# Constant loads spread behind weight chunks, a norm weight applied inside ACT and DVE instructions, and the low-part copies cut differently around the norms

## The chip, the cores and the metric

One core of a Trainium2 chip runs the whole program in one launch. The metric is the device time of one execution in microseconds (us). Engine names are those of the profile: PE is the matrix engine (PEld its weight loads), DVE the vector engine, ACT the scalar engine, POOL the GpSimd engine, SP the engine whose queue issues nearly all transfers.

## What is computed

Four transformer layers over 256 rows of width 1024, all in float32. Cut to the parts that matter here:

```python
def rmsnorm(x, g):                    # two norms a layer in the first two layers
    y = x * rsqrt(mean(x * x, -1) + 1e-6)
    return y * g                      # g: one weight per column

for layer in (0, 1):                  # first block
    x = x + mixer(rmsnorm(x, norm_mix_g[layer]))      # stages 0 and 2
    h = rmsnorm(x, norm_ffn_g[layer])
    x = x + (silu(h @ w1) * (h @ w3)) @ w2            # stages 1 and 3
x = rmsnorm(x, final_norm_g)
for layer in (0, 1):                  # second block
    x = layer_norm(1.414 * x + attention(x), ...)     # stages 4 and 6
    x = layer_norm(1.414 * x + swiglu_2(x), ...)      # stages 5 and 7
```

Every stage is a row of large products of the 256 x K activations with weight matrices read from memory once.

## The kernel before

**Products.** A float32 product is made of three passes over fp32r operands. Each activation and each weight is split into a high part and a low part (low = value minus high), and PE adds high x high, low x high (lines 1020, 1021) and high x low (line 1027) into the PSUM banks `G`.

**Weight chunks.** Weights come in chunks of 128 partitions x 1024 columns (512 KB; three chunks of stage 0 are 840, 840 and 560 wide). Chunk `c` goes through three steps on three engines: SP loads it into one of 4 buffers `raw` (line 905), ACT copies it to one of 6 buffers `whi` (`split`, line 1902, named `HI` in the order), and POOL makes `wlo = raw - whi` (`lo`, line 2156). SP may load chunk `c` when POOL has finished chunk `c - 4`; ACT may split chunk `c` when PE has finished chunk `c - 6`. POOL cuts a chunk into pieces: 256 columns in the even stages, the whole 1024 columns in the odd ones.

```python
cuts = list(range(0, n, 256 if CHUNK_STAGE[c] % 2 == 0 else 1024)) + [n]
```

**Units.** PE's work is numbered in units: one chunk for one half `t` of the rows (two k-tiles, six matmuls of 512 columns). Within a block of output columns PE does all chunks for `t` = 0 and then all of them for `t` = 1.

**The order of everything else** is a table written by hand, `PLAN`, one text for each stage. `66: XG 0 0; SQ 1 0` means that after unit 66 every engine that owns such a step has it next in its queue. A leading minus means that the step belongs to the norm of the stage before. Each engine works strictly in this order, so a step that waits holds up all that stands behind it on its engine, the chunk splits on ACT among them.

**The norms of stages -1 to 2** (before the products of stages 0 to 3), for column half `b` and row half `t`: `RES` (DVE, line 1361) adds the product to `X`; `SQ` (ACT, 1926) sums squares; `XT` (PE, 1041) transposes four 128 x 128 tiles of `X` into the PSUM tensor `A`; `XG` (DVE, 1377) multiplies by the weight column in `CP` and writes to the SBUF buffer `W`; `XH` (ACT, 1943) copies `W` to the high part `xh`; `XL` (DVE, 1385) makes `xl = W - xh`; `SS` (DVE, 1368) and `RS` (ACT, 1885 and 1887) make the reciprocal root, which is applied later, when a product is read out (`EV`, line 1915, or `SI`, line 1956). For the layer norms of stages 4 to 7 there is no `XG`: `AP` (DVE, lines 1409 and 1413) has applied everything to `X` in SBUF, and `XH` and `XL` read `A`. The first unit of a stage waits for `XL 0 0`, the third for `XL 1 0`, the fifth for `XL 0 1`, the seventh for `XL 1 1`.

**Constants.** Behind the load of chunk 7, SP issues seven loads of constants in a row (lines 919 to 925): the two halves of `w1c`, three of `w2c`, the tables `CN` and the decay table in `LC`. `QT` (PE, line 1073) turns the first projected block for its row half, after `EV` of that half.

## Time and profile before

| | |
|---|---|
| time, median of 3 runs | 1406.63 us (1405.68 to 1406.87) |
| the profiled execution's own time | 1401.13 us |
| its span, first to last instruction | 1398.9 us |
| PE busy | 1342.9 us, 96% of the span |
| POOL busy | 1040.7 us, 74% |
| ACT busy | 706.6 us, 51% |
| DVE busy | 410.7 us, 29% |
| mean granted clock of PE | 0.987 of full |

How to read it: the profiled execution took 5.5 us less than the median of the runs (1406.63 less 1401.13), and 2.2 us of it lie outside its span (1401.13 less 1398.9). Times in the rows are counted from the span's start. In a row of the timeline the bracket at the end is the idle time of the engine just before the row, and what ended it.

### The profile page before, as it was taken

To read this page: it belongs to the slowest core of one execution; us is meant where nothing else is said; L and a number is where in the kernel's file an instruction comes from. 1 tells how busy PE (TensorE), PEld (TensorE's weight loads), DVE (VectorE), ACT (ScalarE), POOL (GpSimd) and SP (SyncE) were. 2 spreads that over 40 slices of the span, in tenths; PEclk is the share of its full clock that TensorE was granted. 3 is DMA by queue.
4 is the path that set the end of the run, shared out by engine and by line. 5 is a ranking of instruction groups with operands and counts; after the bars stand their busy time and mean duration, and the time that the engine had idled before them with its cause. 6 is when DMAs were issued, how large, how long until landed. Compare 5 with 4: busy or idle time off the path is not lost.

```text
span 1398.9 us, 19514 instructions
## 1 busy us (share of the span) xinstructions
PE 1342.9 (96%) x7598; PEld 1099.3 (79%) x7598; DVE 410.7 (29%) x785; ACT 706.6 (51%) x1193; POOL 1040.7 (74%) x827
## 2 busy tenths in 40 slices
PE   5999999999999999999999998899999999899997
PEld 4888778888877777888887777688887788688886
...
GB/s 258 100 68 100 125 168 204 182 193 170 193 171 93 121 77 121 194 183 181 181 189 162 185 133 121 139 215 187 195 176 190 192 139 162 111 220 182 191 173 88
DMA packets 63114, 224.90 MB, mean 161 GB/s; under 512 B 7344, under 2 KB 7984, under 8 KB 63024
## 3 DMA queue, kind: packets, MB, share of 16 engines
...
q10 hardware_dynamic: 288, 0.10, 0.0%
...
## 4 chain that ended last, share of the span: by engine, by line
PE 86%; POOL 4%; DVE 3%; ACT 3%; issue 2%; DMA 1%; SPq 0%; DVEq 0%; ACTq 0%
PE G L1020 24%; PE G L1021 24%; PE G L1027 24%; POOL wlo L2156 4%; PE A L1199 1%; PE A L1051 1%; ACT whi L1902 1%; PE A L1133 1%; DMA raw<-in_w_e 1%; PE G L1199 1%; PE A L1169 1%; PE A L1265 1%; DVE X L1409 1%; DVE X L1413 1%; PE G L1133 1%
## 5 line engine op out<-in xcount | busy, mean ns | idle before, releaser
L2156 POOL TENSOR_TENSOR wlo<-raw,whi 128x256 fp32r<-128x256 f32 (+2 forms) x819 | 1031.0, 1296 | 340.2 <-ACT whi L1902 340.2
L1902 ACT ACTIVATE whi<-raw 128x1024 fp32r<-128x1024 f32 x403 | 425.5, 1060 | 353.3 <-PE G L1027 326.6
L1020 PE MATMUL G<-whi,xh 128*128 128x512 f32 (+2 forms) x1200 | 465.8, 392 | 10.9 <-DVE xl L1385 7.1
L1021 PE MATMUL G<-whi,xl 128*128 128x512 f32 (+2 forms) x1200 | 452.7, 381 | 0.0
L1027 PE MATMUL G<-wlo,xh 128*128 128x512 f32 (+2 forms) x1200 | 352.4, 380 | 3.7 <-POOL wlo L2156 3.7
L1020 PEld LDWEIGHTS G<-whi,xh 128*128 128x128 f32 x1200 | 228.6, 190 | 55.7 <-ACT whi L1902 9.7
L1021 PEld LDWEIGHTS G<-whi,xl 128*128 128x128 f32 x1200 | 229.0, 191 | 38.3
L1027 PEld LDWEIGHTS G<-wlo,xh 128*128 128x128 f32 x1200 | 219.5, 190 | 49.7 <-POOL wlo L2156 6.1
L1020 PE MATMUL G<-whi,hh 128*128 128x512 f32 x352 | 139.4, 396 | 0.0
L1021 PE MATMUL G<-whi,hl 128*128 128x512 f32 x352 | 138.8, 394 | 0.0
L1027 PE MATMUL G<-wlo,hh 128*128 128x512 f32 x352 | 110.4, 395 | 0.0
L1361 DVE SCALAR_TENSOR_TENSOR X<-X,G 128x512 f32<-128x512 f32 x32 | 21.6, 685 | 228.8 <-PE G L1027 228.8
L1027 PEld LDWEIGHTS G<-wlo,hh 128*128 128x128 f32 x352 | 66.3, 188 | 15.4
L1021 PEld LDWEIGHTS G<-whi,hl 128*128 128x128 f32 x352 | 66.3, 188 | 15.0
L1020 PEld LDWEIGHTS G<-whi,hh 128*128 128x128 f32 x352 | 66.4, 189 | 15.0
L1426 DVE TENSOR_TENSOR sa<-G,sa 128x512 f32<-128x512 f32 (+1 forms) x24 | 15.5, 646 | 171.0 <-PE G L1027 171.0
L1423 DVE SCALAR_TENSOR_TENSOR sa<-G,SM,sa 128x512 f32<-128x512 f32 (+1 forms) x24 | 16.9, 706 | 163.2 <-PE G L1027 163.2
L1434 DVE TENSOR_TENSOR hl<-A,hh 128x512 fp32r<-128x512 f32 (+1 forms) x48 | 31.1, 647 | 95.7 <-ACT hh L1964 95.7
L1020 PE MATMUL G<-whi,mh 128*128 128x512 f32 x128 | 52.7, 412 | 2.4 <-DVE ml L1441 1.5
L1021 PE MATMUL G<-whi,ml 128*128 128x512 f32 x128 | 50.8, 397 | 0.0
L1027 PE MATMUL G<-wlo,mh 128*128 128x512 f32 x128 | 40.7, 399 | 0.0
L1964 ACT ACTIVATE hh<-A 128x512 fp32r<-128x512 f32 (+1 forms) x48 | 26.5, 552 | 15.2 <-PE A L1051 15.2
...
## 6 DMA issues: line engine op xcount, KB each, us to landing
...
```

The costliest lines, as they stand in the source:

```text
L1020: e.matmul(o, sh[:, kt, xs], whi[h][:, ws], start=u.first and j == 0, stop=False)
L1021: e.matmul(o, sl[:, kt, xs], whi[h][:, ws], start=False, stop=False)
L1027: m = e.matmul(o, sh[:, kt, xs], wlo[h][:, ws], start=False, stop=u.stop and final)
L1133: m = e.matmul(tile[:, at:at + nk], qs[i], ks[i], start=not mask, stop=True, skip_group_check=True)
L1199: m = e.matmul(tile[:, ow * i:ow * i + ow], w[1][0:kp, at:at + 128], vs[i][b], start=b == 0, stop=b == nb - 1)
L1361: e.scalar_tensor_tensor(out=x, in0=x, scalar=1.0 if st < 4 else ALPHA, in1=G[b][:, 512 * t:512 * t + 512], op0=ALU.mult, op1=ALU.add).the ...
L1423: e.scalar_tensor_tensor(out=s_, in0=ps, scalar=rstd[st - 1, t], in1=s_, op0=ALU.mult, op1=ALU.mult).then_inc(S["HM"], 1)
L1426: e.tensor_tensor(s_, ps, s_, ALU.mult).then_inc(S["HM"], 1)
L1434: e.tensor_tensor(hl[sl], ps, hh[sl].bitcast(F), ALU.subtract).then_inc(S["HL"], 1)
L1902: e.activation(whi[c % NH][:, 0:n], raw[c % NR][:, 0:n], ACT.Copy).then_inc(s_hi, 1)
L1964: e.activation(hh[:, 4 * b:4 * b + n, 128 * t:128 * t + 128], ps, ACT.Copy).then_inc(S["HH"], 1)
L2156: m = e.tensor_tensor(wlo[c % NH][:, i:j], raw[c % NR][:, i:j], whi[c % NH][:, i:j].bitcast(F), ALU.subtract)
```

## The change

It has three parts. The seven constant loads are taken apart: one goes behind each of the chunks 7, 8, 10 and 14 and three small ones behind chunk 9. `XG` is gone: in the norms with a weight, ACT reads the transposed tile in PSUM and multiplies by the weight as its per-partition scale, in four instructions of 128 columns, and DVE makes the low part in four instructions (`A * weight - xh`). The table's lines at the norms are written anew for that. And POOL takes chunks 0 to 7 whole, and the first six chunks of every odd stage in pieces of 256.

```diff
@@ PLAN, stage 0 @@
--1: -XT 0 0; -SQ 0 0; -XT 1 0; -XG 0 0; -SQ 1 0; -XG 1 0; -XH 0 0; -SS 0; HI 0; -XL 0 0; HI 1; HI 2
-0: -XH 1 0; -RS 0; -XL 1 0; -XT 0 1; -SQ 0 1; -XT 1 1; -XG 0 1; HI 3
-1: -XG 1 1; -XH 0 1; -XH 1 1; -XL 0 1; -SQ 1 1; -XL 1 1
-2: HI 4; -SS 1; -RS 1; HI 5
+-1: -XT 0 0; -SQ 0 0; -XT 1 0; -XH 0 0; -XH 1 0; -XL 0 0; HI 0; -XL 1 0; HI 1; HI 2
+0: -SQ 1 0; -SQ 0 1; -SS 0; -XT 0 1; HI 3; -XT 1 1
+1: -XH 0 1; -XH 1 1; -XL 0 1; -RS 0; -XL 1 1
+2: -SQ 1 1; HI 4; -SS 1; -RS 1
+3: HI 5
...
@@ SP, behind the load of chunk c @@
                 if c == 7:
+                    e.dma_start(CN[:, 128:NCONST], a["consts"][:, 128:NCONST]).then_inc(d_cn, 16)
+                if c == 8:
                     e.dma_start(w1c[:, 0, :], a["cw1k"]).then_inc(d_cw, 16)
-                    e.dma_start(w1c[:, 1, :], a["cw1v"]).then_inc(d_cw, 16)
+                if c == 9:
                     e.dma_start(w2c[:, 0:64], a["cw2k"]).then_inc(d_cw, 16)
                     e.dma_start(w2c[:, 64:128], a["cw2k"]).then_inc(d_cw, 16)
                     e.dma_start(w2c[:, 128:192], a["cw2v"]).then_inc(d_cw, 16)
-                    e.dma_start(CN[:, 128:NCONST], a["consts"][:, 128:NCONST]).then_inc(d_cn, 16)
+                if c == 10:
+                    e.dma_start(w1c[:, 1, :], a["cw1v"]).then_inc(d_cw, 16)
+                if c == 14:
                     e.dma_start(LC[:, 0:1024], a["ret"]).then_inc(d_ret, 16)
...
@@ DVE @@
-            def x_gain(key):
-                st, b, t = key
-                ps = heads4(A[t][:, 512 * b:512 * b + 512], 4)
-                tmp = heads4(W[t][b][:, 0:512], 4)
-                at = GAIN[st] + 4 * b
-                e.wait_ge(d_cp, 16)
-                e.wait_ge(S["XT"], nth("XT", *key))
-                e.tensor_tensor(tmp, ps, CP[:, at:at + 4].unsqueeze(2).to_broadcast([128, 4, 128]),
-                                ALU.mult).then_inc(S["XG"], 1)
...
+                if norm_kind(st) == "gain":
+                    for j in range(4):
+                        at, kt = GAIN[st] + 4 * b + j, 4 * b + j
+                        m = e.scalar_tensor_tensor(out=xl[:, kt, sl[2]], in0=A[t][:, 512 * b + 128 * j:512 * b + 128 * j + 128],
+                                                   scalar=CP[:, at:at + 1], in1=xh[:, kt, sl[2]].bitcast(F), op0=ALU.mult,
+                                                   op1=ALU.subtract)
...
@@ ACT @@
-                    e.wait_ge(S["XG"], nth("XG", *key))
-                    e.activation(oh, heads4(W[t][b][:, 0:512], 4), ACT.Copy).then_inc(S["XH"], 1)
+                    e.wait_ge(d_cp, 16)
+                    for j in range(4):
+                        at, kt = GAIN[st] + 4 * b + j, 4 * b + j
+                        m = e.activation(xh[:, kt, 128 * t:128 * t + 128], A[t][:, 512 * b + 128 * j:512 * b + 128 * j + 128],
+                                         ACT.Copy, scale=CP[:, at:at + 1])
...
@@ POOL @@
-                cuts = list(range(0, n, 256 if CHUNK_STAGE[c] % 2 == 0 else 1024)) + [n]
+                short = CHUNK_STAGE[c] % 2 == 0 and c >= 8 or CHUNK_STAGE[c] % 2 and c < FIRST[CHUNK_STAGE[c]] + NH
+                cuts = list(range(0, n, 256 if short else 1024)) + [n]
```

Three places of the instruction order follow. The first is SP's queue at the program's start, before the change, from the load of chunk 4 (the number behind `raw` is the buffer's).

```order
L905 DMA raw0<-in_w_e 128x1024
L905 DMA raw1<-in_w_e 128x1024
L905 DMA raw2<-in_w_e 128x1024
L905 DMA raw3<-in_w_e 128x1024
L919 DMA w1c<-in_cw1k 128x1024
L920 DMA w1c<-in_cw1v 128x1024
L921 DMA w2c<-in_cw2k 64x64
L922 DMA w2c<-in_cw2k 64x64
L923 DMA w2c<-in_cw2v 64x64
L924 DMA CN<-in_consts 128x1312
L925 DMA LC<-in_ret 128x1024
L905 DMA raw0<-in_w_e 128x840
```

The same queue with the change (lines count three more there); `in_ret` comes four chunks after the last row.

```order
L908 DMA raw3<-in_w_e 128x1024
L922 DMA CN<-in_consts 128x1312
L908 DMA raw0<-in_w_e 128x840
L924 DMA w1c<-in_cw1k 128x1024
L908 DMA raw1<-in_w_e 128x840
L926 DMA w2c<-in_cw2k 64x64
L927 DMA w2c<-in_cw2k 64x64
L928 DMA w2c<-in_cw2v 64x64
L908 DMA raw2<-in_w_e 128x560
L930 DMA w1c<-in_cw1v 128x1024
L908 DMA raw3<-in_w_e 128x1024
```

Chunks 8 and 9 (the two of 840 columns) now stand ahead of all constants but `CN` and one half of `w1c`.

The second place is DVE at the norm between stages 0 and 1, before the change: residual sums, `XG`, `SS`, the two `XL` of the first row half, the residual sums of the second half and its norm.

```order
L1361 SCALAR_TENSOR_TENSOR X<-X,G1 128x512
L1377 TENSOR_TENSOR W00<-A0,CP 128x512
L1368 TENSOR_TENSOR SM<-SM 128x1
L1377 TENSOR_TENSOR W01<-A0,CP 128x512
L1385 TENSOR_TENSOR xl<-W00,xh 128x4x128
L1385 TENSOR_TENSOR xl<-W01,xh 128x4x128
L1361 SCALAR_TENSOR_TENSOR X<-X,G0 128x512
L1361 SCALAR_TENSOR_TENSOR X<-X,G1 128x512
L1377 TENSOR_TENSOR W10<-A1,CP 128x512
L1377 TENSOR_TENSOR W11<-A1,CP 128x512
```

The same place with the change:

```order
L1368 SCALAR_TENSOR_TENSOR X<-X,G1 128x512
L1387 SCALAR_TENSOR_TENSOR xl<-A0,CP,xh 128x128 x4
L1375 TENSOR_TENSOR SM<-SM 128x1
L1387 SCALAR_TENSOR_TENSOR xl<-A0,CP,xh 128x128 x4
L1368 SCALAR_TENSOR_TENSOR X<-X,G0 128x512
L1368 SCALAR_TENSOR_TENSOR X<-X,G1 128x512
L1387 SCALAR_TENSOR_TENSOR xl<-A1,CP,xh 128x128 x8
L1375 TENSOR_TENSOR SM<-SM 128x1
```

The four `XG` are gone, and each `XL` is four short instructions that read PSUM (`A0`, `A1`) and `xh` instead of the two SBUF tensors `W` and `xh`.

The third place is POOL at the turn from stage 0 to stage 1; the turns into stages 3, 5 and 7 look alike. Before the change, the last chunk of stage 0 and the first ones of stage 1:

```order
L2156 TENSOR_TENSOR wlo4<-raw2,whi4 128x256 x4
L2156 TENSOR_TENSOR wlo5<-raw3,whi5 128x1024
L2156 TENSOR_TENSOR wlo0<-raw0,whi0 128x1024
L2156 TENSOR_TENSOR wlo1<-raw1,whi1 128x1024
L2156 TENSOR_TENSOR wlo2<-raw2,whi2 128x1024
L2156 TENSOR_TENSOR wlo3<-raw3,whi3 128x1024
```

With the change:

```order
L2168 TENSOR_TENSOR wlo5<-raw3,whi5 128x256 x4
L2168 TENSOR_TENSOR wlo0<-raw0,whi0 128x256 x4
L2168 TENSOR_TENSOR wlo1<-raw1,whi1 128x256 x4
L2168 TENSOR_TENSOR wlo2<-raw2,whi2 128x256 x4
L2168 TENSOR_TENSOR wlo3<-raw3,whi3 128x256 x4
L2168 TENSOR_TENSOR wlo4<-raw0,whi4 128x256 x4
L2168 TENSOR_TENSOR wlo5<-raw1,whi5 128x1024
```

Six chunks are in four pieces each, and the seventh is whole again.

## Rows read from the trace of the kernel before

**Rows 1.** Windows: start:end, length; busy us of PE, PEld, DVE, ACT, POOL; PE clock

```profile
180.00:200.00 20.00, 19.32 (x94) 15.64 (x93) 12.83 (x14) 14.05 (x25) 12.44 (x6) 1.00 0.50 155
200.00:366.00 166.00, 166.00 (x798) 138.58 (x797) 22.48 (x30) 78.33 (x89) 141.05 (x60) 1.00 0.61 188
866.00:890.00 24.00, 19.60 (x79) 14.74 (x78) 18.78 (x22) 9.21 (x14) 10.28 (x4) 0.89 0.28 87
1185.00:1215.00 30.00, 23.99 (x101) 18.43 (x100) 18.78 (x22) 12.23 (x17) 13.94 (x7) 0.94 0.33 102
```

**Rows 2.** PE's waits over the whole span: us in total, times, longest

```profile
PE G L1020 <- DVE xl L1385: 7.1, 4, 2.4
PE A L1041 <- DVE X L1413: 5.9, 7, 1.8
PE A L1073 <- ACT PJ L1915: 5.7, 1, 5.7
```

**Rows 3.** Timeline at the start: SP's queue, POOL, ACT and PE

```profile
22.07 0.43 SPq L919 DMA_DIRECT2D w1c<-in_cw1k  x1
...
9.23 23.52 POOL L2156 TENSOR_TENSOR wlo<-raw,whi 128x256 fp32r<-128x256 f32 x32 [8.79 <-ACT whi L1902]
21.73 0.72 PE L1027 MATMUL G<-wlo,xh 128*128 128x512 f32 x2 [1.10 <-POOL wlo L2156]
32.90 0.90 ACT L1902 ACTIVATE whi<-raw 128x840 fp32r<-128x840 f32 x1 [6.13 <-DMA raw<-in_w_e]
35.49 1.11 PE L1073 MATMUL A<-CN,PJ 128*128 128x128 f32 x4 [5.74 <-ACT PJ L1915]
36.26 0.77 PE L1020 MATMUL G<-whi,xh 128*128 128x512 f32 x1
```

**Rows 4.** The weight loads issued between 15 and 40 us, to landing

```profile
DMA to landing us min/median/max: 3.4/3.8/6.8
```

**Rows 5.** POOL's low-part instructions by shape, whole span (busy us, mean ns)

```profile
L2156 POOL TENSOR_TENSOR wlo<-raw,whi 128x1024 fp32r<-128x1024 f32 x264 | 632.0, 2425 | 158.8 <-ACT whi L1902 158.8
L2156 POOL TENSOR_TENSOR wlo<-raw,whi 128x256 fp32r<-128x256 f32 x552 | 398.5, 761 | 181.4 <-ACT whi L1902 181.4
```

**Rows 6.** The tile xl: its DVE instructions, ns min/median/max

```profile
L1385 DVE TENSOR_TENSOR xl<-W,xh x16: 678/1166/2723, 6.8 to 568.5; 128x512 fp32r<-128x512 f32 x16
L1385 DVE TENSOR_TENSOR xl<-A,xh x16: 639/680/693, 751.3 to 1206.0; 128x512 fp32r<-128x512 f32 x16
```

**Rows 7.** Timeline at the turn from stage 0 to stage 1, DVE

```profile
184.41 3.51 DVE L1385 TENSOR_TENSOR xl<-W,xh 128x512 fp32r<-128x512 f32 x2
```

**Rows 8.** Timeline at the start of stage 2

```profile
374.55 38.13 POOL L2156 TENSOR_TENSOR wlo<-raw,whi 128x256 fp32r<-128x256 f32 x48 [1.78 <-ACT whi L1902]
395.38 0.73 PE L1027 MATMUL G<-wlo,xh 128*128 128x512 f32 x2 [1.02 <-POOL wlo L2156]
```

**Rows 9.** Timeline at the turns into stage 5 and stage 7

```profile
871.92 2.58 DVE L1413 SCALAR_TENSOR_TENSOR X<-X,SM,LC 128x512 f32<-128x512 f32 x1 [0.39 <-ACT SM L1887]
877.52 2.08 DVE L1409 SCALAR_TENSOR_TENSOR X<-X,SM,LC 128x512 f32<-128x512 f32 x1
877.63 0.53 PE L1020 MATMUL G<-whi,xh 128*128 128x512 f32 x1 [2.42 <-DVE xl L1385]
1201.66 0.66 PE L1041 MATMUL A<-CN,X 128*128 128x128 f32 x4 [1.83 <-DVE X L1413]
```

**Rows 10.** DVE's norm instructions at the turn into stage 6, ns min/median/max

```profile
L1413 DVE SCALAR_TENSOR_TENSOR X<-X,SM,LC x4: 1037/1042/1048, 1068.1 to 1077.1; 128x512 f32<-128x512 f32 x4
L1409 DVE SCALAR_TENSOR_TENSOR X<-X,SM,LC x4: 744/986/1229, 1067.2 to 1075.7; 128x512 f32<-128x512 f32 x4
```

**Rows 11.** Instructions of 128 columns elsewhere in the kernel, on DVE and on ACT

```profile
L1834 DVE SCALAR_TENSOR_TENSOR MX<-A,SM,AG x10: 341/344/351, 784.8 to 861.9; 128x128 f32<-128x128 f32 x10
...
L2008 ACT ACTIVATE W<-A,SM 128x128 f32<-128x128 f32 x24 | 8.5, 366 | 9.9 <-DVE SM L1524 9.9
409.93 2.64 ACT L2083 ACTIVATE QK<-A 128x512 f32<-128x512 f32 x13
```

More of the change, by code:

```diff
@@ L208 @@
 SPLIT_AT = split_after()
+FIRST = [UNITS[BEGIN[st]].chunk for st in range(8)]
 def frees(kind, key):
@@ L290 @@
 65: RES 0 0; SQ 0 0; XT 0 0; RES 1 0
-66: XG 0 0; SQ 1 0; XT 1 0; XH 0 0; SS 0
-67: XG 1 0; XL 0 0; XH 1 0
+66: XH 0 0; SQ 1 0; XL 0 0; XT 1 0
+67: SS 0; XH 1 0
 68: XL 1 0
-69: RS 0; RES 0 1; XT 0 1; RES 1 1
+69: RES 0 1; RS 0; XT 0 1; RES 1 1
 """,
 """
-0: -SQ 0 1; -XG 0 1; -XT 1 1
-1: -XH 0 1; -XG 1 1; -SQ 1 1; -XL 0 1
-2: -XH 1 1; -SS 1; -RS 1; -XL 1 1
+0: -XH 0 1; -SQ 0 1; -XL 0 1; -XT 1 1
+1: -XH 1 1
+2: -SQ 1 1; -XL 1 1
+3: -SS 1; -RS 1
 4: SI 0 0
@@ L342 @@
 106: RES 0 0; SQ 0 0; XT 0 0
-107: XG 0 0; XH 0 0
+107: XH 0 0
 108: XL 0 0
 110: RES 0 1; SQ 0 1; XT 0 1
-111: XG 0 1; XH 0 1
-112: XL 0 1
+111: XH 0 1; XL 0 1
 128: RES 1 0; SQ 1 0; XT 1 0
-129: XG 1 0; SS 0; XH 1 0
+129: SS 0; XH 1 0
 130: XL 1 0
@@ L354 @@
 0: -RES 1 1; -XT 1 1; -SQ 1 1
-1: -XG 1 1; -SS 1; -XH 1 1
+1: -XH 1 1; -SS 1
 2: -RS 1; -XL 1 1
@@ L412 @@
 75: RES 0 0; SQ 0 0; XT 0 0; RES 1 0
-76: XG 0 0; SQ 1 0; XT 1 0; XH 0 0; SS 0
-77: XG 1 0; XL 0 0; XH 1 0
+76: XH 0 0; SQ 1 0; XL 0 0; XT 1 0
+77: SS 0; XH 1 0
 78: XL 1 0
-79: RS 0; RES 0 1; XT 0 1; RES 1 1
+79: RES 0 1; RS 0; XT 0 1; RES 1 1
 """,
 """
-0: -SQ 0 1; -XG 0 1; -XT 1 1
-1: -XH 0 1; -XG 1 1; -SQ 1 1; -XL 0 1
-2: -XH 1 1; -SS 1; -RS 1; -XL 1 1
+0: -XH 0 1; -SQ 0 1; -XL 0 1; -XT 1 1
+1: -XH 1 1
+2: -SQ 1 1; -XL 1 1
+3: -SS 1; -RS 1
 4: SI 0 0
@@ L700 @@
 SIGNALS = {
-    "EV": "block_evicted", "XT": "x_turned", "XG": "x_gained", "XH": "x_hi", "XL": "x_lo", "RES": "residual_added",
+    "EV": "block_evicted", "XT": "x_turned", "XH": "x_hi", "XL": "x_lo", "RES": "residual_added",
     "SQ": "squares_summed", "SS": "halves_summed", "RS": "rstd_ready", "BN": "bn_stats", "AG": "bn_aggregated",
@@ L1368, in sum_halves @@
                 e.tensor_tensor(norm_sum[key], m[:, 0:1], m[:, 1:2], ALU.add).then_inc(S["SS"], 1)
[L1370 to L1378 removed]
             def x_lo(key):
                 st, b, t = key
[L1382 removed]
                 sl = (slice(None), slice(4 * b, 4 * b + 4), slice(128 * t, 128 * t + 128))
                 e.wait_ge(S["XH"], nth("XH", *key))
[L1385 removed]
+                if norm_kind(st) == "gain":
[4 more added lines that the diff above has]
+                                                   op1=ALU.subtract)
+                else:
+                    m = e.tensor_tensor(xl[sl], heads4(A[t][:, 512 * b:512 * b + 512], 4), xh[sl].bitcast(F), ALU.subtract)
+                m.then_inc(S["XL"], 1)
             def layer_stats(key):
@@ L1854, in lam_ready @@
                 e.tensor_scalar(lam[:, 5:6], lam[:, 4:5], LAM0, None, ALU.add).then_inc(S["P3"], 1)
-            steps = {"RES": residual, "SS": sum_halves, "XG": x_gain, "XL": x_lo, "BN": layer_stats,
+            steps = {"RES": residual, "SS": sum_halves, "XL": x_lo, "BN": layer_stats,
                      "AG": layer_aggregate, "AP": apply_norm, "HM": gate_times_up, "HL": hidden_lo, "ML": mixed_lo,
@@ L1939, in x_hi @@
                 st, b, t = key
-                oh = xh[:, 4 * b:4 * b + 4, 128 * t:128 * t + 128]
+                e.wait_ge(S["XT"], nth("XT", *key))
                 if norm_kind(st) == "gain":
-                    e.wait_ge(S["XG"], nth("XG", *key))
-                    e.activation(oh, heads4(W[t][b][:, 0:512], 4), ACT.Copy).then_inc(S["XH"], 1)
-                else:
-                    e.wait_ge(S["XT"], nth("XT", *key))
-                    e.activation(oh, heads4(A[t][:, 512 * b:512 * b + 512], 4), ACT.Copy).then_inc(S["XH"], 1)
+                    e.wait_ge(d_cp, 16)
[3 more added lines that the diff above has]
+                                         ACT.Copy, scale=CP[:, at:at + 1])
+                else:
+                    m = e.activation(xh[:, 4 * b:4 * b + 4, 128 * t:128 * t + 128],
+                                     heads4(A[t][:, 512 * b:512 * b + 512], 4), ACT.Copy)
+                m.then_inc(S["XH"], 1)
             def gate_silu(key):
```

2 lines of the change are left out of this document (removed).

## The prediction

> **What bounds the kernel now.** I read the windows first, then PE's waits, then the timeline where a wait stands. In the body of an odd stage PE is busy 166.00 of 166.00 us at full clock: there PE alone is the bound, and nothing that this change does to other engines can be seen. Time is lost in short stretches around the norms: PE is idle for 0.68 us in 180:200, for 4.40 us in 866:890 and for 6.01 us in 1185:1215, in the last two with a mean clock of 0.89 and 0.94 [rows 1]. The list of PE's waits names the same places (DVE's `xl`, 7.1 us in 4 waits; DVE's `X` at line 1413, 5.9 us in 7) and one more, 5.7 us at once, where a transpose waits for ACT's eviction [rows 2].
>
> That one lies at the start. PE goes idle at 29.75 us and starts `QT` of the second row half at 35.49, after 5.74 us. The eviction itself takes 0.7 us; ACT comes to it late, since in its queue the splits of chunks 8 and 9 stand ahead, and ACT had sat 6.13 us until the weights of chunk 8 landed, at 32.90. SP began to issue the seven constants at 22.07, and the load of chunk 8 stood behind all of them. POOL matters too: its first eight chunks take 23.52 us, 2.94 each, PE waits 1.10 us for one of them at 21.73, and SP may load chunk 8 only after chunk 4 is through POOL [rows 3]. A load issued in this stretch lands after 3.4 to 6.8 us, half of them within 3.8 [rows 4].
>
> **The start, costed.** POOL takes 2.425 us for a whole chunk and 4 x 0.761 = 3.04 for one in quarters [rows 5]. With whole chunks from 9.23 us on, chunk 5 is through at 9.23 + 6 x 2.42 = 23.8. Then chunk 9 can be loaded, with `CN` and half of `w1c` ahead of it. I take 4.3 us to landing (above the median, since two big constants are still in flight, below the maximum, since five no longer are): 28.1. Then ACT: split 0.90, eviction 0.7, and PE starts `QT` at 29.7. That is 5.8 us earlier than 35.49. PE itself, waiting less for POOL, will be there at about 27.0, so I expect a wait of some 2.7 us left, now on chunk 9. Bounds: landing in 3.4 us gives 28.8 (6.7 us won); POOL unsped (2.94 a chunk, chunk 5 at 26.9) and landing in 6.8 gives 35.3 (0.2 us won). After the wait PE ran at the lower clock, matmuls of 0.77 and then 0.63 us instead of 0.39, which cost 1.25 us over `QT` and one unit; after a shorter wait I count half of that as won, 0.6 (0 to 1.25). Start: **6.4 us** (0.2 to 8.0).
>
> The other constants: `w1c`'s second half now follows chunk 10, landing near 31 us, and is first used near 50; `CN` and `in_ret` have as much cover. They cost nothing unless they hold a chunk, which is the 6.8 us bound.
>
> **The norms with a weight.** DVE's `xl` takes 0.64 to 0.69 us in all 16 cases where it reads PSUM (`A`) and one SBUF tensor, and 0.68 to 2.72, median 1.17, where it reads two SBUF tensors (`W`, `xh`) [rows 6]. At the turn into stage 1 two of the latter take 3.51 us together, while POOL runs 1024-column instructions; the residual sum behind them is late and PE waits [rows 7]. The new `xl` reads `A`, so it leaves the group that waits for POOL.
>
> Price of the new pieces: four DVE ones at up to 0.344 are 1.38 us against 0.7 (`XG`) and 0.68 or more (`XL`). ACT's 128-column ones cost between 0.20 in a row (13 in 2.64 us) and 0.366 each, so 0.8 to 1.5 us against 0.63; I take 1.2 [rows 11]. The chain from `XT` to `XL` goes from 0.7 + 0.63 + 0.7 to about 1.2 + 1.3, half a microsecond longer where nobody held it up, and up to 1.5 shorter where POOL did. At the very start both `XH` (2 x 1.2 after 5.2 us) end at 7.6, ahead of the first weights at 8.1. Elsewhere the first row half's chain ends several us ahead of the stage's first unit, and the second half's has four units (5.5 us) of cover. So only the held-up residual sum counts: 0.7 us in the window 180:200, and the same at the turn into stage 3, which has the same order. Sum **1.4 us** (0 to 1.6).
>
> The Trainium skill, "VectorE: DVE Perf Modes", section "The TRN2 errata", speaks against this part: an instruction pays a fixed latency between instructions, so tiles of 512 elements or more are wanted. The rows show the same (1.38 against 0.68 us on DVE). Read by the rule alone, the half microsecond of longer chain would be lost at each of the three turns, 1.5 us off the sum (1395.1); by the rows it falls where PE does not wait.
>
> At the start of stage 2 POOL runs 48 quarters without a pause in 38.13 us, 3.18 a chunk, and PE, which needs one each 2.73 (two units of 1.36), waits 1.02 us at 395.38 [rows 8]. With four fewer collisions POOL gets there sooner: **0.7 us** (0 to 1.4).
>
> **The turns into stages 5 and 7** keep their instructions; POOL's pieces beside them shrink. Now line 1413 takes 2.58 and line 1409 2.08 us, PE waits 2.42 for the first `xl`, and in stage 7 another 1.83 for `AP 1 0` [rows 9]. The turn into stage 6 shows the same instructions beside quarters: 1.04 for line 1413, 0.74 to 1.23 for line 1409 [rows 10]. With 1.1 for each, the first `AP` ends 1.5 us earlier, but the next sum needs PE's last unit, so `xl` comes only 0.35 earlier. `AP 1 0` ends 2.7 us earlier, before PE has done its first two units; `AP 0 1` and `AP 1 1` follow, the last beside POOL still. Walked through, the third unit starts at 884.3 instead of 886.2 in stage 5 and at 1203.5 instead of 1205.4 in stage 7: **3.7 us** in both (2.5 to 6). PE's clock is low for 8 or 9 matmuls at each turn, at 0.2 us apiece; with less idle time I count half of one, **0.8** (0 to 3.4).
>
> Cost of quarters: six chunks in four stages at 0.6 more each are 15 us of POOL time. At the turn into stage 1 the fourth chunk's low part is done near 190 and used at 194.5; so it is hidden. If that cover of 4.5 us were gone, PE would be paced by 3.18 instead of 2.73 for six chunks, 2.7 us a stage.
>
> **Sum.** 6.4 + 1.4 + 0.7 + 3.7 + 0.8 = 13.0 us. The profiled execution would go from 1401.13 to 1388.1; its difference to the runs' median (5.5 us) stays, so the runs: **1393.6 us**.
>
> **Rivals.** (a) *The wait at the start stays*: chunk 9 lands late since `CN` and `w1c` fill the engines. For it: 6.8 us has happened. Then 1 to 3 us are won there, in all 7 to 9: 1398.5. (b) *More comes back*: PE's clock stays up at the start and at both turns, and chunk 9 lands in 3.4: 17 to 20 us, 1388. (c) *Slower*: the weight column `CP` lies in SBUF; if as a scalar it counts as a second SBUF input, every piece of `xl` waits for a POOL instruction. At the start eight pieces at 2.42 put `XL 1 1` at 35 us, and `QT` at 39 instead of 35.5 (+3.5); at the turns into stages 1 and 3 eight pieces at 0.75 take 6 us where 3.5 were taken (+2.3 each), in stage 2 +1; less 4.5 from stages 5 and 7: +4.6, 1411.2. It decides once more than about half of the pieces wait. Against it: line 1834, with PSUM, a scalar in SBUF and one SBUF tensor, takes 0.341 to 0.351 in ten of ten [rows 11]. The Trainium skill, "SBUF — State Buffer", section "Who interferes with whom", says that a vector instruction with two SBUF inputs and a GpSimd one that reads SBUF shut each other out for a whole instruction, and one with at most one SBUF input does not; whether a scalar column counts it leaves open. If not, (c) falls away. (d) *Nothing*: stage 0 has later waits on DVE and ACT, and what the start wins could be taken back there, with quarters eating the rest: 1405.
>
> **Chances.** My forecast (10 to 17 us) 0.60; (a) 0.18; (b) 0.10; (c) 0.05; (d) 0.07. Runs of this kernel differ by 0.1%, so 0.2% (2.8 us) is what can be told from no change. Faster 0.88, same 0.07, slower 0.05. The range takes in (a) and most of (b): 1387.5 to 1400.5.
>
> **What would show it.** Right: `QT`'s wait falls from 5.74 to some 3 us and is ended by chunk 9's split; POOL's first eight take 19.4 us; no `xl` over 0.4 us a piece; PE's wait for line 1361 gone; line 1413 at 1.0 to 1.3 us in stages 5 and 7, with PE idle there 2.5 and 4 us instead of 4.4 and 6.0. Wrong: new PE waits for `wlo` early in odd stages, for `xl` at a first unit, or for `w1c`.

## The result

The changed kernel took 1392.71 us (median of 4 runs, 1389.81 to 1395.68), the kernel before 1406.16 beside it (4 runs, 1403.09 to 1406.87): a ratio of 0.9885, 95% interval 0.9849 to 0.9921, 13.45 us. Six more runs of the changed kernel later (`e12_after_again`) had a median of 1394.42, ratio 0.9934 (0.9909 to 0.9958). Over all ten the median is 1394.1; the three later sets of the kernel before have medians of 1406.32, 1405.74 and 1404.34. By these medians the change is worth 10 to 13 us (the two intervals leave 6 to 21), and single runs of one kernel differ by up to 15 us. Part of that spread turned out to have a cause of its own, in the body of a stage that the change does not touch.

The first part of the page of the profiled execution (1391.12 us):

```profile
span 1389.3 us, 19642 instructions
PE 1338.4 (96%) x7598; PEld 1098.7 (79%) x7598; DVE 394.4 (28%) x817; ACT 713.0 (51%) x1241; POOL 1044.5 (75%) x875
```

### The profile page after: what moved, and what is told of

It reads as the page before. It is cut to its first block, busy times and chain, and to the rows that moved or that the text cites. A ratio compares the mean times of both kernels' runs of the same rounds, so it can differ in the third digit from the quotient of the medians.

```text
span 1389.3 us, 19642 instructions
## 1 busy us (share of the span) xinstructions
PE 1338.4 (96%) x7598; PEld 1098.7 (79%) x7598; DVE 394.4 (28%) x817; ACT 713.0 (51%) x1241; POOL 1044.5 (75%) x875
## 4 chain that ended last, share of the span: by engine, by line
PE 88%; POOL 3%; DVE 3%; ACT 3%; DMA 2%; issue 2%; SPq 0%; DVEq 0%; ACTq 0%
PE G L1027 25%; PE G L1028 24%; PE G L1034 24%; POOL wlo L2168 3%; PE A L1206 1%; PE A L1058 1%; ACT whi L1909 1%; PE A L1140 1%; DMA raw<-in_w_e 1%; PE G L1206 1%; PE A L1272 1%; DMA raw<-in_w_b 1%; PE A L1176 1%; DVE X L1416 1%; PE G L1140 1%
## 5 line engine op out<-in xcount | busy, mean ns | idle before, releaser
L2168 POOL TENSOR_TENSOR wlo<-raw,whi 128x256 fp32r<-128x256 f32 (+1 forms) x867 | 1034.8, 1230 | 326.9 <-ACT whi L1909 326.8
```

What stands on the lines that cost most here:

```text
L2168: m = e.tensor_tensor(wlo[c % NH][:, i:j], raw[c % NR][:, i:j], whi[c % NH][:, i:j].bitcast(F), ALU.subtract)
```

## The profile after

**The start**, in the timeline of SP, POOL, ACT and PE, against [rows 3]:

```profile
18.61 0.43 SPq L922 DMA_DIRECT2D CN<-in_consts  x1
20.59 0.33 SPq L908 DMA_DIRECT2D raw<-in_w_e  x1
20.96 1.09 SPq L924 DMA_DIRECT2D w1c<-in_cw1k  x1
22.94 0.33 SPq L908 DMA_DIRECT2D raw<-in_w_e  x1
...
8.80 18.83 POOL L2168 TENSOR_TENSOR wlo<-raw,whi 128x1024 fp32r<-128x1024 f32 x8 [8.36 <-ACT whi L1909]
...
27.09 0.90 ACT L1909 ACTIVATE whi<-raw 128x840 fp32r<-128x840 f32 x1 [1.91 <-DMA raw<-in_w_e]
29.90 0.90 ACT L1909 ACTIVATE whi<-raw 128x840 fp32r<-128x840 f32 x1 [1.91 <-DMA raw<-in_w_e]
30.71 0.67 ACT L1922 ACTIVATE PJ<-G,SM 128x512 f32<-128x512 f32 x1
...
31.43 1.12 PE L1080 MATMUL A<-CN,PJ 128*128 128x128 f32 x4 [4.93 <-ACT PJ L1922]
32.20 0.78 PE L1027 MATMUL G<-whi,xh 128*128 128x512 f32 x1
32.78 0.63 PE L1028 MATMUL G<-whi,xl 128*128 128x512 f32 x1
```

The last two loads of `raw` are chunks 8 and 9. Chunk 9 is issued at 22.94, with `CN` and half of `w1c` ahead of it, and its split starts at 29.90, when it has landed, 6.9 us later. The eviction stands behind that split, and PE's transpose behind the eviction, after 4.93 us instead of 5.74. PE then runs at the lower clock (0.78 and 0.63 us a matmul), as before.

Counted from POOL's first instruction, `QT` starts at 22.63 us instead of 26.26, so 3.6 us are won there. In this pair of executions nothing of it is left at the end of stage 0, where the first residual sum comes 170.8 us after POOL's first instruction in both. From `QT` to PE's next wait the changed kernel takes 14.83 us at a mean clock of 0.80, the kernel before 13.31 us at 0.90 (1.5 us back); the transpose at line 1070 waits 2.22 us where it waited 1.61 (0.6 back); and from there to the residual sum it takes 12.38 us at 0.87 against 10.85 at 1.00 (1.5 back).

**The norms**, in the list of the instructions that make `xl` (the three durations are the shortest, the median and the longest, in ns) and in the windows of the first turn, against [rows 6] and [rows 1]:

```profile
L1387 DVE SCALAR_TENSOR_TENSOR xl<-A,CP,xh x64: 339/343/352, 6.5 to 561.5; 128x128 fp32r<-128x128 f32 x64
```

```profile
172.00:192.00 20.00, 20.00 (x98) 16.48 (x97) 7.58 (x21) 13.67 (x33) 14.49 (x22) 1.00 0.45 138
```

All 64 pieces take 0.34 or 0.35 us. PE has no idle time left at the turn into stage 1 (20.00 of 20 us busy).

**The turn into stage 5**, PE and DVE in the timeline, against [rows 9]:

```profile
866.62 0.92 DVE L1420 SCALAR_TENSOR_TENSOR X<-X,SM,LC 128x512 f32<-128x512 f32 x1 [0.39 <-ACT SM L1894]
...
871.79 1.03 DVE L1416 SCALAR_TENSOR_TENSOR X<-X,SM,LC 128x512 f32<-128x512 f32 x1
872.94 1.03 DVE L1420 SCALAR_TENSOR_TENSOR X<-X,SM,LC 128x512 f32<-128x512 f32 x1
873.90 1.22 DVE L1416 SCALAR_TENSOR_TENSOR X<-X,SM,LC 128x512 f32<-128x512 f32 x1
...
871.90 0.47 PE L1027 MATMUL G<-whi,xh 128*128 128x512 f32 x1 [2.22 <-DVE xl L1391]
876.31 0.66 PE L1048 MATMUL A<-CN,X 128*128 128x128 f32 x4 [0.95 <-DVE X L1420]
878.57 0.66 PE L1048 MATMUL A<-CN,X 128*128 128x128 f32 x4 [1.61 <-DVE X L1420]
```

Line 1420 (1413 before) takes 0.92 to 1.03 us where it took 2.58. PE still waits 4.78 us over the turn, no less than before (4.40 idle), since the six instructions of `AP 1 0`, `0 1` and `1 1` take 1.03 to 1.22 each, one behind the other: the first two are shorter than they were, the last four longer (0.74 or 0.75 before). The mean clock over the 24 us of the turn is 0.93 instead of 0.89. In the windows of stage 7's turn PE idles 3.50 us where it idled 6.01:

```profile
1176.00:1206.00 30.00, 26.50 (x115) 21.10 (x114) 15.80 (x22) 13.44 (x19) 21.54 (x24) 0.94 0.39 121
```

## The experiments

Twelve runs, of which the last is the changed kernel again. To see past the spread I read each profile by six sections (differences of start times in the timeline, us). The first goes from POOL's first instruction to the first residual sum of stage 0's end. The next ones end at the first residual sum of the second column half in stage 1, at the first residual sum of stages 2, 3 and 5, and at that of the second column half in stage 7. "Stage 2" thus covers the turn into stage 2 and its body. A number in the table is of one execution.

```
kernel              start+0  stage 1  stage 2  stage 3  4 and 5  6 and 7
before               170.8    191.9    181.3    160.4    320.7    351.5
after                170.8    191.0    178.2    159.4    319.2    348.9
e1_consts            167.3    191.9    181.3    160.4    320.8    351.8
e2_norms             170.6    191.0    191.6    159.4    323.3    351.8
e3_cuts              169.8    191.0    187.5    159.4    320.3    349.0
e4_late              165.2    191.0    188.3    159.4    320.1    349.5
e5_late_ev           164.5    191.0    191.8    159.5    320.2    349.2
e6_no_turn_cuts      168.7    191.0    181.9    159.4    322.9    351.6
e7_first_quarters    168.0    191.0    183.9    159.5    319.2    348.8
e8_psum_q            167.0    191.0    177.2    159.4    320.3    349.2
e9_q_both            167.3    191.0    177.6    159.5    319.2    348.7
e10_before_psum_q    172.8    191.9    185.2    160.4    322.2    351.5
e11_all              166.9    191.0    177.6    159.5    320.1    348.3
e12_after_again      169.0    191.0    191.9    159.5    320.2    349.0
```

### The three parts alone: e1_consts, e2_norms, e3_cuts

Each is the kernel before with one part of the change: the `if c == 7` to `if c == 14` blocks of loads; the norm steps with their `PLAN` rows; the `short` line with `FIRST`.

> The kernel before with only the loads of the constants moved (CN behind chunk 7, w1c's first half behind 8, w2c behind 9, w1c's second half behind 10, ret behind 14). Theory T1 (the wait at the start is ended by chunk 9, which lands late since constants are in flight with it; POOL's quarters feed that too): POOL's first eight still take 23.5 us, SP's load of chunk 8 goes out at about 23.0 and of chunk 9 at about 25.5 to 26, it lands 5 to 7 us later, QT starts at 32.5 to 33.5, so 2 to 3 us of the 5.74 come back: 1404 against 1406.2 (2 us faster). Rival (the old stand behind seven constants was the whole wait): QT at 30 to 31, 4.5 to 5.5 us faster. Rival (nothing is won without whole chunks on POOL): within 0.5 us at QT.

> The kernel before with only the norms with a weight changed (no XG; ACT scales by the column, DVE's xl reads PSUM with the column as its scalar; the order list goes with it). Theory T2a (xl no longer waits for POOL because its wide input is in PSUM): pieces of xl of 0.28 to 0.36 us also beside POOL's 1024-column instructions, the turns into stages 1 and 3 shorter by 0.5 to 0.9 us each, stage 2's wait for wlo gone; 1403 to 1404.5. Rival T2b (the gain at those turns came from POOL's quarters alone): four pieces take 3 us and more beside POOL, the turns stay as they were or get longer, 1406 or more. Nothing else moves: QT at 35.5, turns into stages 5 and 7 as before.

> The kernel before with only POOL's low parts cut differently (first eight chunks whole, first four chunks of an odd stage in quarters). Theory T3 (quarters carry the turns into stages 5 and 7): line 1413 at 1.0 to 1.3 us there, those two turns together 4 to 5 us shorter; at the start POOL's first eight take 19 us, chunk 8 can be issued earlier but the seven constants stand ahead of it, so QT comes 1 to 3 us earlier; at the turns into stages 1 and 3 xl still reads two SBUF tensors but beside quarters, 1.0 to 1.2 us instead of 1.75, so 0.5 to 1 us each. Sum 6 to 9 us: 1397 to 1400. Rival (clock spells made most of the difference at the turns): 1 to 2 us at the turns, 1402 to 1404.

| kernel | median us (range, runs) | ratio to before, 95% |
| --- | --- | --- |
| e1_consts | 1402.98 (1396.45 to 1409.80, 12) | 0.9968, 0.9943 to 0.9993 |
| e2_norms | 1405.60 (1399.86 to 1412.79, 12) | 0.9989, 0.9965 to 1.0014 |
| e3_cuts | 1399.32 (1393.23 to 1403.28, 12) | 0.9941, 0.9918 to 0.9964 |

The three ratios add up to 14.3 us, the differences of the medians to 11.1, against the 10 to 13 of the whole; each ratio is uncertain by some 3.5 us, and the interval of `e2_norms` includes 1, so the times can't tell whether the parts add up. (The expectations speak of four chunks in quarters at an odd stage; the code makes it six.) `e1_consts` has its gain in the first section, 3.5 us against the profile of before: PE waits 2.75 us at `QT`, and then stays at the higher clock (0.48 us for the first matmul). Timeline of PE and of POOL in it:

```profile
31.08 0.66 PE L1077 MATMUL A<-CN,PJ 128*128 128x128 f32 x4 [2.75 <-ACT PJ L1919]
31.50 0.48 PE L1024 MATMUL G<-whi,xh 128*128 128x512 f32 x1
...
7.81 28.23 POOL L2160 TENSOR_TENSOR wlo<-raw,whi 128x256 fp32r<-128x256 f32 x40 [7.37 <-ACT whi L1906]
```

POOL began 1.42 us sooner in this execution than in that of [rows 3]; counted from POOL's first instruction `QT` starts at 23.3 us instead of 26.3. That is the 2 to 3 us that T1 gave. But chunk 9 did not land in 5 to 7 us, though `CN` and half of `w1c` stand ahead of it here as well. Its queue for 20 to 31 us (KB each, median us from issue to landing):

```profile
raw<-in_w_e SPq DMA_DIRECT2D x2, 420.0 KB, 3.8
```

POOL's first chunks are still in quarters, and so SP issues the chunks 2.78 us apart and not 2.35 as in `after`. `CN`, chunk 8, `w1c`'s half and chunk 9 have 656 + 420 + 512 + 420 = 2008 KB and go out over two such distances. My estimate from that: 437 GB/s are asked for at 2.35 us, 370 at 2.78. The transfers moved 365 GB/s in 26 to 31 us of `after`, with a busy share of 1.01. So the late landing in the changed kernel takes both, the constants in flight and POOL's faster pace; `e7_first_quarters`, which has the constants of the changed kernel and POOL's quarters, lands the two chunks after 3.7 us.

The other two parts bring `QT` forward as well: it starts at 24.3 us after POOL's first instruction in `e2_norms`, which was expected to leave it where it was, and at 24.2 in `e3_cuts`. Each part alone wins 1.9 to 3.0 us at `QT`, and all three together 3.6.

`e2_norms` and `e3_cuts` each shorten the turns into stages 1 and 3 by 0.9 to 1.0 us, and so does the change with both: these two gains are one and the same. The instructions that make `xl`, first in `e2_norms`, then in `e3_cuts`:

```profile
L1383 DVE SCALAR_TENSOR_TENSOR xl<-A,CP,xh x64: 339/343/354, 6.4 to 574.6; 128x128 fp32r<-128x128 f32 x64
```

```profile
L1386 DVE TENSOR_TENSOR xl<-W,xh x16: 677/1047/2858, 6.9 to 568.6; 128x512 fp32r<-128x512 f32 x16
```

Beside POOL's whole chunks the new form takes 0.354 us at most: here a weight column as scalar did not count as a second SBUF input, and theory T2a holds (the time, 1405.60, did not come down to its 1403 to 1404.5). The old form takes up to 2.86 (at the start, beside whole chunks) and 1.83 for two beside quarters, where PE does not wait for them. Stages 4 to 7 gain only in `e3_cuts`, by 0.4 and 2.5 us against the profile of before; its time, 1399.32, is the 1397 to 1400 of T3.

What I had not expected stands in the column of stage 2: 191.6 us in `e2_norms`, 187.5 in `e3_cuts`, 181.3 before, though neither touches its body. Here is one place in it, first in `e3_cuts`, then in `after`:

```profile
398.32 0.69 DVE L1733 SCALAR_TENSOR_TENSOR A<-PJ,A 128x512 f32<-128x512 f32 x1
398.93 10.64 DVE L1734 SCALAR_TENSOR_TENSOR PJ<-PJ,W 128x512 f32<-128x512 f32 x1
```

```profile
398.94 0.70 DVE L1739 SCALAR_TENSOR_TENSOR A<-PJ,A 128x512 f32<-128x512 f32 x1
399.54 1.02 DVE L1740 SCALAR_TENSOR_TENSOR PJ<-PJ,W 128x512 f32<-128x512 f32 x1
```

One product of two SBUF tensors, the last operation of the step `FF`, takes 10.64 us in the one and 1.02 in the other.

### e4_late and e5_late_ev: what is left of the wait at the start

`e4_late` puts `CN` behind chunk 10, `w1c`'s first half behind chunk 11, and `w2c` and `w1c`'s second half behind chunk 12:

```diff
-                if c == 7:
+                if c == 10:
                     e.dma_start(CN[:, 128:NCONST], ...)
-                if c == 8:
+                if c == 11:
                     e.dma_start(w1c[:, 0, :], a["cw1k"])
-                if c == 9:
+                if c == 12:
                     e.dma_start(w2c[:, 0:64], a["cw2k"])
...
```

> The changed kernel with the constants later still: CN behind chunk 10, w1c's first half behind 11, w2c and w1c's second half behind 12, so that no constant stands ahead of chunks 8 to 10. Theory T1 (what is left of the wait is chunk 9 in flight with CN and w1c): chunk 9 is issued at about 22.5 and lands within 4.5 us, at 27; its split ends at 28, the eviction at 28.8, QT starts at 28.8 to 29.2 instead of 31.43, a wait of 1.5 to 2.5 instead of 4.93: 2 to 3 us faster than the changed kernel, 1390 against 1392.7 where the clock is alike. Rival (chunk 9 lands late whatever else is in flight, since it is SP's issue after POOL's chunk 5 and the queue's own depth): QT at 31 to 31.5, 1392.7. Rival (a constant comes too late now): a new wait for CN or w1c after 40 us, the lead lost again.

Measured: 1391.87 us (1387.23 to 1397.32, 6 runs), ratio 0.9890 (0.9857 to 0.9923). ACT's and PE's timelines in it:

```profile
26.47 0.90 ACT L1908 ACTIVATE whi<-raw 128x840 fp32r<-128x840 f32 x1 [1.27 <-DMA raw<-in_w_e]
27.28 0.67 ACT L1921 ACTIVATE PJ<-G,SM 128x512 f32<-128x512 f32 x1
...
28.00 0.91 PE L1079 MATMUL A<-CN,PJ 128*128 128x128 f32 x4 [1.93 <-ACT PJ L1921]
28.55 0.78 PE L1026 MATMUL G<-whi,xh 128*128 128x512 f32 x1
```

The wait is 1.93 us instead of 4.93, and `QT` starts 3.0 us sooner counted from POOL's first instruction (19.63 against 22.63). The queue's answers, for 20 to 30 us in `e4_late` and 20 to 31 in `after` (KB each, median us from issue to landing):

```profile
raw<-in_w_e SPq DMA_DIRECT2D x2, 420.0 KB, 4.0
```

```profile
raw<-in_w_e SPq DMA_DIRECT2D x2, 420.0 KB, 6.6
w1c<-in_cw1k SPq DMA_DIRECT2D x1, 512.0 KB, 7.0
```

At this pace of POOL chunks 8 and 9 land after 4.0 us with no constant ahead of them, and after 6.6 with `CN` and `w1c` in flight. T1 is shown for `QT`, and no wait for a constant came in its place. The first section has 165.2 us, 3.4 less than the five executions that have the start of the changed kernel (168.6 on the mean). The times do not tell whether it stays: the median is 0.8 us below that of the changed kernel's first four runs and 2.2 below that of all ten, less than these few runs can tell apart. The profiled execution spent 188.3 us in stage 2, for a cause that comes below.

`e5_late_ev` moves one step of the order as well:

```diff
-8: EV 0 1; QT 1 @1
+7: EV 0 1
+8: QT 1 @1
```

> e4_late with the eviction EV 0 1 one unit earlier in stage 0's order, so that on ACT it stands ahead of chunk 9's split. Theory T1 (after e4_late, ACT's order is what is left: QT at 19.6 us after POOL's start, behind chunk 9's split): QT of the second row half starts 1 to 1.5 us sooner still and PE's wait there falls from 1.93 to 1 or less. The time goes with it by 1 us or not at all, since the next units wait for the same chunk: 1390 to 1392. Rival (shorter idle keeps PE's clock up as well): 1388 to 1389, no low clock at 25 to 35 us.

Measured: 1390.20 us (1384.87 to 1399.88, 6 runs), ratio 0.9906 (0.9875 to 0.9937). `QT` starts at 26.47 us with no wait, 2.1 us sooner than in `e4_late` counted from POOL's first instruction, and PE stays at full clock until 35. That is the sign of the rival, but the time is T1's, 1390 to 1392. The stall has moved to 41 us, on PE and ahead of it on ACT:

```profile
41.20 0.29 PE L1093 MATMUL G<-CN,PJ 128*64 128x128 f32 x1 [3.43 <-ACT PJ L1922]
...
39.42 1.06 ACT L1909 ACTIVATE whi<-raw 128x1024 fp32r<-128x1024 f32 x1 [2.72 <-DMA raw<-in_w_e]
```

In 35 to 40 us PE is busy 2.77 of 5 us, with the transfer engines at 0.98. ACT waits for a weight chunk again, and the section is only 0.7 us shorter than in `e4_late`. That the constants, late now, take the transfers of the chunks that PE has caught up with fits these rows; no run has them later still.

### e6_no_turn_cuts and e7_first_quarters: which of POOL's cuts count

`e6_no_turn_cuts` drops the second half of the condition, `e7_first_quarters` the `c >= 8`:

```diff
-short = CHUNK_STAGE[c] % 2 == 0 and c >= 8 or CHUNK_STAGE[c] % 2 and c < FIRST[CHUNK_STAGE[c]] + NH
+short = CHUNK_STAGE[c] % 2 == 0 and c >= 8
```

> The changed kernel without the quarters of the first four chunks of odd stages; all else as changed. Theory T3 (the quarters carry the turns into stages 5 and 7): line 1416 (1413 before) at 2.6 us there again, waits at both turns as before, 4 to 5 us of the lead gone; xl at the turns into stages 1 and 3, now with its wide input in PSUM, stays at 0.28 to 0.36 us a piece beside whole instructions, so those two keep 1 to 1.9 us. 1396 to 1398. Rival (at these turns PE's clock, not DVE, made the difference): 1393 to 1394.

> The changed kernel with chunks 0 to 7 in quarters again. Theory T1b (whole chunks at the start let chunks 8 and 9 be loaded sooner): POOL's first eight take 22 to 23.5 us instead of 18.8, the loads of chunks 8 and 9 go out 2 to 3 us later, QT starts 2 to 2.5 us later against the start of POOL, 1394 to 1395. Rival (chunk 9's slow landing behind the constants hides it): QT at the same place within 0.5 us, 1392.7.

`e6_no_turn_cuts`: 1399.05 us (1395.74 to 1406.83, 12 runs), ratio 0.9955 (0.9932 to 0.9979). Stages 4 and 5 together have 322.9 us and stages 6 and 7 351.6, as in the four kernels without these quarters (320.7 to 323.3 and 351.5 to 351.8); the turns into stages 1 and 3 keep their gain (191.0 and 159.4). Its DVE timeline at the turn into stage 5:

```profile
869.04 2.58 DVE L1420 SCALAR_TENSOR_TENSOR X<-X,SM,LC 128x512 f32<-128x512 f32 x1 [0.38 <-ACT SM L1894]
...
874.64 2.08 DVE L1416 SCALAR_TENSOR_TENSOR X<-X,SM,LC 128x512 f32<-128x512 f32 x1
876.83 2.66 DVE L1420 SCALAR_TENSOR_TENSOR X<-X,SM,LC 128x512 f32<-128x512 f32 x1
```

T3 is shown, and 1399.05 is 1 us above its range.

`e7_first_quarters`: 1391.84 us (1385.92 to 1396.92, 6 runs), ratio 0.9900 (0.9867 to 0.9933), first section 168.0 us, within the five of the whole chunks (167.0 to 170.8). Its `QT` starts at 23.3 us after POOL's first instruction, 0.6 later, where T1b gave 2 to 2.5 and the rival at most 0.5, so the rival is nearer. PE waited only 1.12 us there, after 2.76 at an earlier transpose, and its clock stayed up. Chunk 9 goes out 4.2 us later than in `after` and lands after 3.35 us instead of 6.88, so it is there only 0.6 us later. Whole chunks at the start are worth nothing that can be told. This one execution is no clean test, though, since DVE stood still in it at the start:

```profile
17.05 5.66 DVE L1375 TENSOR_TENSOR SM<-SM 128x1 f32<-128x1 f32 x1
...
22.74 0.30 ACT L1892 ACTIVATE SM<-SM 128x1 f32<-128x1 f32 x1 [4.79 <-DVE SM L1375]
```

What holds such an instruction up comes next.

### e8, e9, e10 and e12: the product in stage 2

`e8_psum_q` lets ACT write the factor into the half of the PSUM tile `A` that is free by then:

```diff
-e.activation(q_, q_, ACT.Exp, scale=-1.0).then_inc(S["FE"], 1)
+e.activation(m, q_, ACT.Exp, scale=-1.0).then_inc(S["FE"], 1)
...
-e.scalar_tensor_tensor(out=fq, in0=fq, scalar=-(128 ** -0.5), in1=q_, op0=ALU.mult,
+e.scalar_tensor_tensor(out=fq, in0=fq, scalar=-(128 ** -0.5), in1=m, op0=ALU.mult,
```

`e10_before_psum_q` is the same edit on the kernel before. `e9_q_both` is `e8_psum_q` with DVE's second clamp of the step `FB` (its expectation calls it the first) written to PSUM as well (`L` instead of `q_`), and ACT's first exponential of it moved from `FE` to `FA`. `e12_after_again` is the changed kernel itself.

> The changed kernel with one operand moved in stage 2: the last factor of DVE's fourth operation of FF (a product of two SBUF tensors) is written by ACT into a PSUM slot that is free by then. In e2_norms, e3_cuts and e4_late that operation took 10.64 us instead of 1.02 beside POOL's unbroken quarters and PE then waited up to 7.9 us. Theory T5 (this lockout falls in some executions and not in others, and makes most of the spread of the times): the operation takes 0.7 us, no run above 1393, spread 5 us or less, median 1389 to 1391; the profile has no wait over 2 us for it. Rival (the spread is from spells of low clock alone): spread and median as the changed kernel's, 1390 to 1396, 1392.7.

> The kernel before with the same one operand of stage 2 in PSUM. Theory T5 (lockout in some executions): times of before spread from 1400.5 to 1413.8 in 29 runs; with the operand in PSUM the upper part goes, 1399 to 1405, median 1402 to 1403 against 1406.3 (4 us faster, since half of the executions lost 6 to 8). Rival (clock spells): median 1406, spread the same.

> e8_psum_q with the first clamp of stage 2's FB written to PSUM too (in e10_before_psum_q its SBUF to SBUF form took 5.44 us instead of 0.41); ACT's first exponential of it moves ahead, from FE to FA. Theory T5 (what is left of the upper times of e8_psum_q, 1394.6 and 1397.0 of six, is this second lockout): all runs within 1384 to 1390, median 1387. Rival (the upper times come from low clock after idle stretches): one run in three still above 1393.

> The changed kernel itself, unaltered, for more of its executions. Theory T5 (lockouts in stage 2 in some executions): two clusters, some runs at 1388 to 1392 and some at 1394 to 1399, median 1391 to 1394; if the profiled execution is of the upper ones, one DVE instruction in 390 to 425 us takes over 2 us. Rival: one cluster.

| kernel | median us (range, runs) | ratio to before, 95% |
| --- | --- | --- |
| e8_psum_q | 1387.20 (1385.46 to 1396.96, 6) | 0.9892, 0.9861 to 0.9924 |
| e10_before_psum_q | 1403.80 (1398.37 to 1408.02, 12) | 0.9982, 0.9961 to 1.0004 |
| e9_q_both | 1389.54 (1386.55 to 1390.59, 4) | 0.9892, 0.9875 to 0.9909 |
| e12_after_again | 1394.42 (1390.60 to 1403.74, 6) | 0.9934, 0.9909 to 0.9958 |

The profiled execution of `e12_after_again` is the same program as `after` and has a span of 1401.9 us, not 1389.3. Its DVE, ACT, POOL and PE in stage 2:

```profile
397.73 10.66 DVE L1740 SCALAR_TENSOR_TENSOR PJ<-PJ,W 128x512 f32<-128x512 f32 x1
...
401.46 0.67 ACT L1922 ACTIVATE PJ<-G,SM 128x512 f32<-128x512 f32 x1
408.43 0.60 ACT L2079 ACTIVATE lfh<-A 128x512 fp32r<-128x512 f32 x1 [6.30 <-DVE PJ L1740]
...
393.27 14.57 POOL L2168 TENSOR_TENSOR wlo<-raw,whi 128x256 fp32r<-128x256 f32 x21
...
411.05 1.30 PE L1259 MATMUL A<-CN,PJ 128*128 128x128 f32 x5 [7.88 <-DVE PJ L1750]
```

The rows give the chain. DVE's product arrives while POOL goes from quarter to quarter with no pause, and does not get in. ACT, at its next step, waits for that product, and its chunk splits stand behind the wait. So POOL runs out of split chunks, pauses at 393.27 + 14.57 = 407.84, and the product ends at 408.39. In all five executions with such a product it ends 0.54 to 0.56 us after POOL's pause begins, and it takes 10.64 to 10.67 us each time: it lasts as long as POOL's store of work. The same shows outside stage 2. In `e1_consts` a copy of one SBUF tensor, at the start, ends as POOL's 28.23 us end (7.81 + 28.23 = 36.04):

```profile
25.96 10.17 DVE L1499 CAST IB<-CN 128x128 bf16<-128x128 f32 x1 [9.15 <-DMA CN<-in_consts]
```

No wait of PE stands behind that one. The 5.66 us in `e7_first_quarters` end at 22.71, POOL pauses at 22.69, and ACT's next split had stood behind them. In `e12_after_again` PE waits 7.88 us behind the product and starts again at the lower clock, as its windows show (the PE clock is the third number from the end):

```profile
400.00:405.00 5.00, 3.17 (x13) 1.99 (x11) 5.00 (x1) 1.64 (x2) 5.00 (x8) 1.00 0.64 193
405.00:410.00 5.00, 0.00 (x0) 0.00 (x0) 4.70 (x4) 1.57 (x4) 2.84 (x5) 0.52 0.59 175
410.00:415.00 5.00, 3.95 (x15) 3.79 (x16) 3.51 (x11) 4.15 (x16) 0.00 (x0) 0.50 0.14 55
```

Of the ten profiled executions with this product in SBUF (before, after, e1 to e7, e12) five have it at 10.64 to 10.67 us (e2, e3, e4, e5, e12), and their stage 2 takes 187.5 to 191.9 us; the other five have 1.01 or 1.02 us and 178.2 to 183.9. The second product of the same line takes 2.58 and 2.62 us in two of these, `e6_no_turn_cuts` and `e7_first_quarters` (1.2 to 1.3 in the other three), and PE then waits 3.2 us for the step behind it instead of 1.8 or 1.9: their stage 2 has 181.9 and 183.9. With the operand in PSUM it takes 0.68, in `e9_q_both`:

```profile
395.89 0.68 DVE L1740 SCALAR_TENSOR_TENSOR PJ<-PJ,A 128x512 f32<-128x512 f32 x1
```

and stage 2 takes 177.2 to 177.6 us in e8, e9 and e11. `e10_before_psum_q` shows that it isn't the only such place. An instruction that reads and writes SBUF alone (0.45 us for the same line in the profile of before) took

```profile
407.39 5.44 DVE L1717 TENSOR_SCALAR W<-PJ 128x512 f32<-128x512 f32 x1
```

Here PE waited 6.29 us, and stage 2 took 185.2. `e9_q_both` moves that one too, and its four runs cover 4 us, where the changed kernel's ten cover 14; its median, 1389.54, is above the 1387 expected.

For the profiled executions T5 is shown. For the times it is borne out in part. The ten runs of `e8_psum_q` and `e9_q_both` have a median of 1388.0 us, the ten of the changed kernel 1394.1. But `e8_psum_q` was to have no run above 1393 and a spread of 5 us, and has 1394.61 and 1396.96 and a spread of 11.5; the second place may explain them, but no profile shows it. `e10_before_psum_q` was to win 4 us and has 1.9, with an interval that includes 1. `e12_after_again` was to fall into two groups, and its six times (1390.60, 1393.26, 1393.85, 1394.99, 1397.70, 1403.74) do not. So how much of the spread comes from blocked instructions, and how much from clock spells, stays open, and four runs are few.

### e11_all

`e5_late_ev` and `e9_q_both` together.

> e5_late_ev and e9_q_both together: later constants, the earlier eviction, and both operands of stage 2 in PSUM. If their gains add: the start gives 1 to 3 us over the changed kernel and stage 2 another 4 to 5 in the median: 1384 to 1387 against 1392.7. Rival (the start's gain is given back to the clock, as in e4_late): 1387, as e9_q_both.

Measured: 1387.11 us (1386.53 to 1392.49, 5 runs), ratio 0.9881 (0.9864 to 0.9898). That is the fastest version by its ratio, though its interval and that of `e9_q_both` overlap, and it is at the upper end of 1384 to 1387, as the rival has it. Its first section, 166.9 us, is 0.4 below `e9_q_both`'s: the start's gain was mostly given back, at the wait that `e5_late_ev` showed (3.84 us at 41.20 here).

## Why the prediction was right, and where not

The time, 1392.71 against 1393.6, came out as forecast, and so did where the time is won; the size of the largest term did not, and the sum is right partly by luck. For each term, sections of kernels with that part of the change are set against those without it. One section is one execution, so the means are uncertain by 1 us or more.

- **Start, 6.4 us: measured 3.3** (171.8 on the mean in before and e10, 168.6 in after, e6, e8, e9 and e12), and with `e2_norms`, whose constants are as before, 2.8. In the profiled pair it is 0.0, since all of `QT`'s lead went back to waits and clock before stage 0's end. The step that failed is "I take 4.3 us to landing". Chunk 9 landed after 6.9, just beyond the upper bound, and the wait was 4.93 us, not 2.7; the term for the clock (0.6) fell away, since PE ran at the lower clock after it, for longer than before. This is the mechanism of rival (a), at this place. `e4_late` confirms the rest of the sum: with a landing in 3.9 us the wait is 1.93. Also wrong was the part of POOL: it took 18.83 us for eight chunks (19.4 forecast), and this pace, which the sum counts as a gain, is what the late landing took besides the constants. `e1_consts` without it has as good a first section, 167.3. That the gain could be taken back later in stage 0 stood in rival (d), and at the start that is in part what happened.
- **Norms with a weight, 1.4: measured 1.9** (0.9 at each of the two turns), above the 1.6 that was its upper bound. No piece over 0.354 us, PE's wait for line 1361 gone, rival (c) ruled out. But the gain is not the norms' alone: POOL's quarters without the new norms have it too (`e3_cuts`). That a longer chain costs nothing held: no PE wait for `xl` at a first unit of stages 1 and 3.
- **Start of stage 2, 0.7: measured 3.1** in the pair (181.3 to 178.2). Some 2.9 us of it is a spell of lower clock at 485 to 497 us that before has and after does not (windows of 5 us: 0.88, 0.50, 0.94). An idle stretch of the same length stands just ahead of it in both (1.85 us at line 1265, 1.86 at 1272), and of the fourteen profiled executions eight have such a spell, with and without the change. So it isn't the change's, and what decides it stays open; without it 0.2 is left. The other two profiled executions of the changed code in stage 2 without a blocked first product, e6 and e7, have 181.9 and 183.9, with a spell and a second product of 2.6 us. The 1.02 us wait for the low part, which the term was about, is gone: PE's waits for POOL are 0.7 us at most in the changed kernel, in stage 2 0.41.
- **Turns into stages 5 and 7, 3.7 and 0.8 for the clock: measured 4.8** (322.0 to 319.9 and 351.7 to 349.0 on the means; in the pair 1.5 and 2.7). The size is right; the walk through the turn was not. PE's idle time fell to 3.5 us in stage 7 (4 forecast), but in stage 5 its waits are 4.78 us, not 2.5 and not less than before: six `AP` instructions of 1.03 to 1.22 us, not 1.1 with the later ones free of POOL, hold the transposes.
- **The spread.** "Runs of this kernel differ by 0.1%" rested on three runs. 63 more ran from 1399.20 to 1414.06, 1.1%. The measured terms, 3.3 + 1.9 + 3.1 + 4.8 = 13.1, are near the 13.0 of the forecast partly by luck: the first term was 3 too high, and a clock spell of 2.9 us that only the profile of before has makes up for it. The difference of the two profiled executions is 10.0 us (1401.13 to 1391.12).
